# Two expert tables copied into one with 8 KB rows, fetched by one gather a pair

## The chip, the cores and the metric

The kernel runs on one core of one Trainium2 chip. The metric is the device time of one execution in microseconds; 3 runs of the kernel before are given. A core has five engines with streams of instructions of their own that meet only at semaphores: TensorE (PE, matmuls), VectorE (DVE), ScalarE (ACT), GpSimd (POOL) and SyncE (SP, which only issues transfers here). 16 DMA engines move the data.

## The reference

One sequence of 512 tokens of width 1024 in float32 goes through two blocks of layers. What is computed, in the order of the kernel:

- retention and forgetting attention, each `x = x + gate * mixer(h)`, with a modulation from `c`, and a final norm;
- a second block: `h = rms_norm(x)`, stick-breaking attention and a gated delta rule on projections of `h`, both gated and merged into `x`;
- the experts, product-key retrieval, the part that the change is about:

```python
q = einsum('bsd,de->bse', h, w_q)                    # 8 heads x 256
s1, s2 = scores of q's halves against keys1, keys2   # 128 keys each
v1, i1 = top_k(s1, 16); v2, i2 = top_k(s2, 16)
vals, c = top_k(v1[..., :, None] + v2[..., None, :], 16)
expert = i1[c // 16] * 128 + i2[c % 16]              # of 16384
gate = softmax(vals)
u = u_tab[expert]; v = v_tab[expert]                 # rows of 1024
x = x + sum_e gate_e * gelu(h . u_e) * v_e           # 128 experts a token
```

Each of the 512 tokens fetches 128 rows of the table u and 128 of the table v, 4096 B each: 537 MB in all. Both tables have 16384 rows (67 MB each).

## The kernel before

All of the kernel's stages follow one another on the whole sequence: retention, forgetting, stick breaking, the inputs of the delta rule, the delta rule, gates, merge, experts. Weights of the projections come in chunks of 512 columns, two halves of 1 MB each. `load` (L191) has SP wait until DVE has split the half before (`w_split`) and then issues the transfer into `raw[h]`; ACT makes the high part (L214), DVE the low part (L219), and PE multiplies with both (L277). `load_chunks` (L197) is a loop on SP where there are more than 4 chunks. In the blocks of the attention proper (line 1493 and on, line 1735 and on) SP has nothing to issue; in the delta rule's block only the masks (L2202).

The experts are `peer` (L2684). Tokens lie on the 128 partitions, 4 tiles of 128 tokens; the 128 experts of a token are 16 groups of 8, so there are 64 groups, and every gather fetches, for one expert place `k`, one row per partition, by an index on that partition (`eidx`). Before, a gather fetches a row of u or a row of v, 512 KB, so a group takes 16 gathers, and the stage 1024, all issued by POOL through `gather_row` (L2721). For each group:

- DVE makes 8 dot products of a u row with the token's h (L2928), 1024 wide, into `dots`;
- ACT applies gelu (L3045), DVE multiplies by the gate (L2945), ACT spreads the 8 weights into 8 diagonal matrices (L3049);
- PE multiplies each diagonal by the v row, two matmuls of 512 columns an expert, and sums all 128 experts of a tile in PSUM (`weigh`, L2830, in part a loop of rounds). Each expert counts `v_used`.

There are 16 slots for u rows and 16 for v rows, two groups of each; `u_row` and `v_row` (L2819, L2822) say where they lie, in tiles that earlier stages have left. POOL issues the 8 u gathers of group g once DVE has made the dots of group g-2 (`dot_done`), and then the 8 v gathers of group g once PE has used the rows of group g-2 (`v_used`), one after the other (`gather`, L3075). For the first two groups it waits instead for what lies in the tiles: the x stored, the last weights split, the last projection done, the last scores read.

Between the dots of the groups DVE also chooses the keys and experts of later groups (`top_keys`, `top_pairs`, `experts`, `softmax`) up to the 52nd group or so; these stand in the order of lines 2968 to 2996. The dots of the last group are made in three segments (4, 2 and 2). After each tile of tokens `add_rows` (L2948) adds the sum to x, and PE waits for that before the next tile.

## Time and profile before

| | us |
|---|---|
| median of 3 runs | 3343.18 (3341.9 to 3343.9) |
| profiled execution | 3344.73 |
| its span | 3342.9 |
| busy: PE | 2809.0 (84%) |
| busy: DVE | 1849.4 (55%) |
| busy: ACT | 884.3 (26%) |
| busy: POOL | 1216.9 (36%) |
| DMA, mean over the span | 211 GB/s |

The span reaches from the first to the last instruction; the execution's own time lies 1.8 us above it. Busy times are sums over the whole span, and the kernel's stages differ much, so they say little of one stage: the slices and windows do. L12 is line 12 of the kernel. What "idle before" is ascribed to is inferred from semaphores; where a DMA is named that ended long ago, the name says nothing. In a timeline PE's ends are modelled.

### The profile page before, as it was taken

What the parts mean: (1) busy time and instruction counts of PE and PEld (TensorE: products, weight loads), DVE (VectorE), ACT (ScalarE), POOL (GpSimd) and SP (SyncE); (2) the same over time, 40 slices, a digit from 0 to 9 for tenths busy, and PEclk for the clock granted to TensorE, in tenths of its full rate; (3) what the DMA queues carried; (4) which work ended last, traced back from release to release, by engine and by line L of the source; (5) the groups of instructions that cost most, each with busy time, mean ns of one, the idle gap of its engine ahead of it and who ended that gap; (6) DMA issues with size and microseconds to landing.
All of it is one profiled execution on the core that took longest, in us unless ns stands there. A gap on an engine that the chain in (4) does not pass through costs nothing. (4 is left out here: it accounts for less than half of the span.)

```text
span 3342.9 us, 31046 instructions
## 1 busy us (share of the span) xinstructions
PE 2809.0 (84%) x10832; PEld 1865.1 (56%) x10832; DVE 1849.4 (55%) x3524; ACT 884.3 (26%) x1621; POOL 1216.9 (36%) x1236
## 2 busy tenths in 40 slices
PE   6999999999899999999999786766776667757777
PEld 5888587765677677898778632222332222323323
DVE  4761544244534564556344676656667666757443
ACT  2112322514446564324223211111111111111111
POOL 0000210000202241540001466666666666666665
PEclk7999999999999999999999898878888878878878
DMA  6452123200221123003233799999999999999998
GB/s 235 154 186 88 63 82 96 88 26 1 87 90 63 52 89 119 1 1 115 88 111 110 264 352 370 365 370 390 371 368 364 380 368 386 353 374 382 367 369 312
DMA packets 228772, 706.47 MB, mean 211 GB/s; under 512 B 23188, under 2 KB 25492, under 8 KB 227735
## 3 DMA queue, kind: packets, MB, share of 16 engines
q0 software_dynamic: 147456, 536.94, 41.8%
q1 hardware_dynamic: 81176, 167.76, 14.6%
q8 instruction: 77, 1.26, 0.2%
q14 instruction: 63, 0.52, 0.0%
HBM read 694.13 MB, written 10.49 MB: 211 GB/s over the span
## 5 line engine op out<-in xcount | busy, mean ns | idle before, releaser
L2836 PE MATMUL work_banks<-rows_over_split,sig 128*128 128x512 f32 x1024 | 518.9, 661 | 265.7 <-issue 191.6
L2836 PEld LDWEIGHTS work_banks<-rows_over_split,sig 128*128 128x128 f32 x1024 | 214.6, 212 | 562.0 <-issue 482.3
L219 DVE TENSOR_TENSOR weights_low<-weights_raw,weights_high 128x2048 fp32r<-128x2048 f32 x108 | 250.5, 2320 | 430.4 <-ACT weights_high L214 420.9
L2836 PE MATMUL work_banks<-weights_raw,sig 128*128 128x512 f32 x512 | 266.5, 678 | 155.3 <-issue 90.9
L2928 DVE CUSTOM_DVE_ANT_0 proj_banks<-rows_over_parts,work_banks 128x1024 f32<-128x1024 f32 x256 | 309.1, 1245 | 155.5 <-DMA rows_over_parts<-in_peer_u_dram,eidx 74.6
L277 PE MATMUL proj_banks<-h_low,weights_high 128*128 128x512 f32 x896 | 357.9, 399 | 27.9 <-DVE weights_low L219 9.1
L214 ACT CAST weights_high<-weights_raw 128x2048 fp32r<-128x2048 f32 x108 | 206.0, 1907 | 610.9 <-PE proj_banks L277 582.7
L277 PE MATMUL proj_banks<-h_high,weights_low 128*128 128x512 f32 x896 | 352.7, 394 | 0.0
L277 PE MATMUL proj_banks<-h_high,weights_high 128*128 128x512 f32 x896 | 352.5, 393 | 0.0
L2722 POOL DMA_INDIRECT rows_over_split<-in_peer_v_dram,eidx x256 | 241.6, 944 | 156.2 <-issue 71.9
L2836 PEld LDWEIGHTS work_banks<-weights_raw,sig 128*128 128x128 f32 x512 | 109.3, 219 | 310.5 <-issue 245.3
L3045 ACT ACTIVATE coef<-dots 128x8 f32<-128x8 f32 x63 | 13.1, 209 | 985.2 <-issue 569.5
L2722 POOL DMA_INDIRECT rows_over_parts<-in_peer_u_dram,eidx x256 | 239.8, 937 | 79.8 <-issue 71.4
L3049 ACT ACTIVATE sig<-shape_consts,coef 128x128 f32<-128x128 f32 x504 | 154.0, 388 | 222.9 <-DVE coef L2945 117.8
L277 PEld LDWEIGHTS proj_banks<-h_low,weights_high 128*128 128x128 f32 x896 | 170.5, 190 | 66.2 <-issue 21.9
L2928 DVE CUSTOM_DVE_ANT_0 proj_banks<-u_rows_first,work_banks 128x1024 f32<-128x1024 f32 x128 | 154.8, 1254 | 69.5 <-DMA u_rows_first<-in_peer_u_dram,eidx 54.4
L277 PEld LDWEIGHTS proj_banks<-h_high,weights_low 128*128 128x128 f32 x896 | 170.8, 191 | 37.0 <-issue 1.9
L277 PEld LDWEIGHTS proj_banks<-h_high,weights_high 128*128 128x128 f32 x896 | 170.6, 190 | 36.3
L2836 PE MATMUL work_banks<-v_rows,sig 128*128 128x512 f32 x384 | 177.7, 612 | 8.0 <-issue 8.0
L277 PE MATMUL proj_banks<-weights_high,h_low 128*128 128x512 f32 x448 | 177.2, 395 | 0.0
L277 PE MATMUL proj_banks<-weights_high,h_high 128*128 128x512 f32 x448 | 174.4, 389 | 0.0
L277 PE MATMUL proj_banks<-weights_low,h_high 128*128 128x512 f32 x448 | 174.3, 389 | 0.0
(490 smaller groups left out, 4934.5 us busy)
## 6 DMA issues: line engine op xcount, KB each, us to landing
weights_raw<-in_w_in_dram SPq DMA_DIRECT2D x36, 1024.0 KB, 4.9
weights_raw<-in_ret_w_in_dram SPq DMA_DIRECT2D x24, 1024.0 KB, 5.2
ret_gate<-in_mod_w_dram SPq DMA_DIRECT2D x20, 1024.0 KB
weights_raw<-in_fox_w_in_dram SPq DMA_DIRECT2D x16, 1024.0 KB, 5.2
weights_raw<-in_ret_w_out_dram SPq DMA_DIRECT2D x8, 1024.0 KB, 5.2
weights_raw<-in_peer_w_q_dram SPq DMA_DIRECT2D x8, 1024.0 KB, 5.3
ret_v<-in_mod_w_dram SPq DMA_DIRECT2D x4, 1024.0 KB
weights_raw<-in_fox_w_out_dram SPq DMA_DIRECT2D x4, 1024.0 KB, 5.1
```

Source lines behind the costliest of these rows:

```text
L214: nc.scalar.copy(whi[h][:, :, :], raw[h][:, :, :]).then_inc(high_ready[h], 1)
L219: nc.vector.tensor_tensor(wlo[h][:, :, :], raw[h][:, :, :], whi[h][:, :, :].bitcast(F32), ALU.subtract).then_inc(w_split[h], 1)
L277: last = nc.tensor.matmul(out_tile, lhs, rhs, start=(start and j == 0), stop=(stop and j == 2))
L2722: return nc.gpsimd.indirect_dma_start(out=to, out_offset=None, in_=table, in_offset=bass.IndirectOffsetOnAxis(ap=eidx[:, t, k:k + 1].bitca ...
L2836: last = nc.tensor.matmul(pa[:, half, :], diag[:, s, e, :], v_row(s, e)[:, half * CW:(half + 1) * CW], start=(first and e == 0), stop=(las ...
L2928: nc.vector.tensor_tensor_reduce(out=trash[:, e % 2, :], in0=u_row(g % 2, e), in1=hp, scale=1.0, scalar=0.0, op0=ALU.mult, op1=ALU.add, ac ...
L3045: nc.scalar.activation(coef[:, g % 2, :], dots[:, g % 2, :], ACT.Gelu).then_inc(gelu_done, 1)
L3049: nc.scalar.activation(diag[:, g % 2, e, :], ident, ACT.Copy, scale=coef[:, g % 2, e:e + 1]).then_inc(diag_ready, 1)
```

## The change

Both tables are copied by DMA, DRAM to DRAM, into a third, `joined_rows`, whose row i is the u row and the v row of expert i side by side, 8192 B. The copy is 128 pieces of 256 rows, 1 MB each. SP issues them (`join_rows`): one behind each half of a weight load (but not in the first 8 chunks of retention), one after each step of the attention blocks and some of the delta rule's, where SP's stream has new waits for the steps of these stages. The loop of `load_chunks` is unrolled for that. POOL waits for all 128 before the first gather.

One gather then fetches both rows of an expert, 1 MB, 512 gathers in all. There are 16 slots of 8 KB per partition, in the same tiles; a slot is free again when PE has used its v half, for DVE's dots have read its u half before that. PE's weighing is written out without a loop, and its waits for `v_loaded` and ACT's waits for `v_used` go.

```diff
 
+
+JOIN_PIECES = 128
+JOIN_ROWS = PEER_KEYS * PEER_KEYS * 2 // JOIN_PIECES
...
+    joined = nc.dram_tensor("joined_rows", [PEER_KEYS * PEER_KEYS, 2 * D], F32, kind="Internal").ap()
+    state = {"g": 0, "joined": 0}
 
 
 
-    def load(sp, src, c, g):
+    def join_rows(sp, pieces=1):
+
+        for piece in range(state["joined"], min(state["joined"] + pieces, JOIN_PIECES)):
+            rows = slice(piece // 2 * JOIN_ROWS, (piece // 2 + 1) * JOIN_ROWS)
+            table = a["peer_v_2" if piece % 2 else "peer_u_2"][0]
+            sp.dma_start(joined[rows, piece % 2 * D:(piece % 2 + 1) * D], table[rows, :]).then_inc(rows_joined, 16)
+            state["joined"] = piece + 1
+
+    def load(sp, src, c, g, join=True):
 
         for h in range(2):
             sp.wait_ge(w_split[h], g + 1)
             sp.dma_start(raw[h][:, :, :], src(c, h)).then_inc(w_loaded[h], 16)
+            if join:
+                join_rows(sp)
 
     def load_chunks(sp, src, n, then=None):
 
         g0 = state["g"]
-        if n <= 4:
-            for c in range(1, n):
-                load(sp, src, c, g0 + c)
-        else:
-            with sp.Fori(0, n - 1) as i:
-                load(sp, src, i + 1, i + (g0 + 1))
+        for c in range(1, n):
+            load(sp, src, c, g0 + c)
         if then is not None:
             load(sp, then, 0, g0 + n)
...
                             late_unit(u)
                         for c in range(1, n):
-                            load(sp, ret_in_src, c, g0 + c)
+                            load(sp, ret_in_src, c, g0 + c, join=c >= 8)
                             if 4 <= c < 8:
                                 for u in range(units_before[c], units_before[c + 1]):
...
+                    @block.sync
+                    def _(sp):
+                        for m in range(PAIRS):
+                            sp.wait_ge(o_full, m + 1)
+                            join_rows(sp)
+
                     @block.tensor
...
                 with nc.Block() as block:
+                    @block.sync
+                    def _(sp):
+                        for h in range(H):
+                            sp.wait_ge(z_full, B * (h + 1))
+                            join_rows(sp)
+                            sp.wait_ge(o_full, h + 1)
+                            join_rows(sp)
+
                     @block.tensor
                     def _(pe):
...
                     sp.dma_start(masks[:, :, :], a["inv_masks"]).then_inc(masks_loaded, 16)
+                    for h in range(H):
+                        sp.wait_ge(products_full, h + 1)
+                        join_rows(sp)
+                    for g in range(NG):
+                        for lv in range(LV):
+                            sp.wait_ge(cs_ready, nth(g, lv, HG - 1))
+                            join_rows(sp)
+                    for n in range(0, TT * H, 4):
+                        sp.wait_ge(vn_full, n + 1)
+                        join_rows(sp)
                     sp.wait_ge(z_put, 16)
 
                 @block.gpsimd
...
-        u_loaded = [[sem(f"u_loaded{s}_{b}") for b in range(GE)] for s in range(2)]
-        v_loaded = [[sem(f"v_loaded{s}_{b}") for b in range(GE)] for s in range(2)]
+        pair_loaded = [[sem(f"pair_loaded{s}_{b}") for b in range(GE)] for s in range(2)]
         ur0 = sbuf(st, "u_rows_first", [P, GE // 2, D])
...
-
-        def gather_row(to, table, t, k):
+        def gather_pair(to, t, k):
             return nc.gpsimd.indirect_dma_start(
-                out=to, out_offset=None, in_=table,
+                out=to, out_offset=None, in_=joined,
                 in_offset=bass.IndirectOffsetOnAxis(ap=eidx[:, t, k:k + 1].bitcast(U32), axis=0))
 
         def top16(values, scratch, out_v, out_i):
...
             dots = sbuf(st2, "dots", [P, 2, GE])
             coef = sbuf(st2, "coef", [P, 2, GE])
-            diag = spare[:, 2:6, :].rearrange("p j (e n) -> p j e n", e=4).rearrange("p (s j) e n -> p s (j e) n", s=2)
+            diag = spare[:, 0:4, :].rearrange("p j (e n) -> p j e n", e=4).rearrange("p (s j) e n -> p s (j e) n", s=2)
             trash = pb[:, :, :].rearrange("p (e b) n -> p e (b n)", e=2)
             hp = pa[:, 2:4, :].rearrange("p b n -> p (b n)")
 
+            def pair(s, e):
+
+                flat = lambda ap: ap.rearrange("p b n -> p (b n)")
+                if s == 0 and e < 4:
+                    return flat((ur0 if e < 2 else x)[:, 2 * (e % 2):2 * (e % 2) + 2, :])
+                if s == 0 and e < 6:
+                    return flat(raw[e % 2][:, :, :])
+                if e >= 6:
+                    return flat((over_split[:, 2:4, :], over_split[:, 6:8, :], vr[:, 0:2, :],
+                                 spare[:, 4:8, :])[2 * s + e - 6])
+                row = (0, 4, 2, 6, 0, 4)[e]
+                return flat((over_parts if e < 4 else over_split)[:, row:row + 2, :])
+
             def u_row(s, e):
-                return over_parts[:, (0, 1, 4, 5, 2, 3, 6, 7)[e], :] if s else first_u_row(e)
+                return pair(s, e)[:, 0:D]
 
             def v_row(s, e):
-                if s == 0:
-                    return raw_row(e) if e < GE // 2 else over_split[:, (2, 3, 6, 7)[e - GE // 2], :]
-                if e < 4:
-                    return over_split[:, (0, 1, 4, 5)[e], :]
-                return vr[:, e - 4, :] if e < GE - 1 else spare[:, 6:8, :].rearrange("p b n -> p (b n)")
+                return pair(s, e)[:, D:2 * D]
 
             with nc.Block() as block:
-                def weigh(pe, r, s, t, first, last_of_tile):
+                def weigh(pe, t, g):
 
                     for e in range(GE):
-                        pe.wait_ge(diag_ready, r * (2 * GE) + (t * NG * GE + s * GE + e + 1))
-                        pe.wait_ge(v_loaded[s][e], r * 16 + 16 * (t * NG // 2 + 1))
+                        pe.wait_ge(diag_ready, (t * NG + g) * GE + e + 1)
                         for half in range(2):
-                            last = nc.tensor.matmul(pa[:, half, :], diag[:, s, e, :],
-                                                    v_row(s, e)[:, half * CW:(half + 1) * CW],
-                                                    start=(first and e == 0),
-                                                    stop=(last_of_tile and e == GE - 1))
+                            last = nc.tensor.matmul(pa[:, half, :], diag[:, g % 2, e, :],
+                                                    v_row(g % 2, e)[:, half * CW:(half + 1) * CW],
+                                                    start=(g == 0 and e == 0),
+                                                    stop=(g == NG - 1 and e == GE - 1))
                         last.then_inc(v_used, 1)
 
...
@@ -2890,13 +2926,8 @@
                     for t in range(TT):
                         if t:
                             pe.wait_ge(y_added, t)
-                        weigh(pe, 0, 0, t, True, False)
-                        weigh(pe, 0, 1, t, False, False)
-                        with rounds(pe, NG // 2 - 2) as r:
-                            for s in range(2):
-                                weigh(pe, r + 1, s, t, False, False)
-                        weigh(pe, NG // 2 - 1, 0, t, False, False)
-                        weigh(pe, NG // 2 - 1, 1, t, False, True)
+                        for g in range(NG):
+                            weigh(pe, t, g)
 
                 @block.vector
                 def _(dve):
...
                     def scores_of(t, g, rows=(0, GE)):
 
                         for e in range(*rows):
-                            dve.wait_ge(u_loaded[g % 2][e], 16 * ((t * NG + g) // 2 + 1))
+                            dve.wait_ge(pair_loaded[g % 2][e], 16 * ((t * NG + g) // 2 + 1))
 
                             dve.wait_ge(dot_done, (t * NG + g) * GE + (PRE + e - 1))
...
@@ -3022,6 +3053,12 @@
                         nc.scalar.copy(sc[:, t, 4 * n - 4:4 * n, :],
                                        pa[:, t, :].rearrange("p (f c) -> p f c", c=P)).then_inc(sc_ready, 1)
 
+                    def diagonals(n_of, lo=0, hi=GE):
+
+                        for e in range(lo, hi):
+                            nc.scalar.activation(diag[:, n_of % 2, e, :], ident, ACT.Copy,
+                                                 scale=coef[:, n_of % 2, e:e + 1]).then_inc(diag_ready, 1)
+
                     for t in range(TT):
                         for g in range(NG):
                             n_of = t * NG + g
...
@@ -3031,11 +3068,7 @@
                                     nc.scalar.activation(coef[:, g % 2, lo:hi], dots[:, g % 2, lo:hi], ACT.Gelu
                                                          ).then_inc(gelu_done, 1)
                                     act.wait_ge(coef_ready, n_of + 1 + segment)
-                                    if segment == 0:
-                                        act.wait_ge(v_used, n_of * GE + GE)
-                                    for e in range(lo, hi):
-                                        nc.scalar.activation(diag[:, g % 2, e, :], ident, ACT.Copy,
-                                                             scale=coef[:, g % 2, e:e + 1]).then_inc(diag_ready, 1)
+                                    diagonals(n_of, lo, hi)
                                 continue
                             if n_of == 3:
                                 exponentials(0, 1)
...
@@ -3044,54 +3077,30 @@
                             act.wait_ge(dot_done, n_of * GE + (PRE + GE))
                             nc.scalar.activation(coef[:, g % 2, :], dots[:, g % 2, :], ACT.Gelu).then_inc(gelu_done, 1)
                             act.wait_ge(coef_ready, n_of + 1)
-                            act.wait_ge(v_used, n_of * GE + GE)
-                            for e in range(GE):
-                                nc.scalar.activation(diag[:, g % 2, e, :], ident, ACT.Copy,
-                                                     scale=coef[:, g % 2, e:e + 1]).then_inc(diag_ready, 1)
+                            diagonals(n_of)
 
                 @block.gpsimd
                 def _(pool):
                     pool.wait_ge(eidx_ready, 1)
-                    for e in range(GE):
-                        if e == GE // 2:
-                            pool.wait_ge(x_put, 16)
-                        gather_row(first_u_row(e), u_tab, 0, e).then_inc(u_loaded[0][e], 16)
-                    for e in range(GE // 2):
-                        if e % 2 == 0:
-                            pool.wait_ge(w_split[e // 2], state["g"] + n + 1)
-                        gather_row(raw_row(e), v_tab, 0, e).then_inc(v_loaded[0][e], 16)
-                    pool.wait_ge(first_used, state["g"] + n + 1)
-                    for e in range(GE // 2, GE):
-                        gather_row(v_row(0, e), v_tab, 0, e).then_inc(v_loaded[0][e], 16)
-                    for e in range(GE):
-                        if e == GE // 2:
-                            pool.wait_ge(tile_full[3], state["g"] + n + 1)
-                        gather_row(u_row(1, e), u_tab, 0, GE + e).then_inc(u_loaded[1][e], 16)
-                    for e in range(GE):
-                        if e == GE // 2:
-                            pool.wait_ge(s_full, 4 * n)
-                        gather_row(v_row(1, e), v_tab, 0, GE + e).then_inc(v_loaded[1][e], 16)
-
-                    def gather(table, g, s, used, loaded, rows=(0, GE)):
-
-                        t, first = g // NG, (g % NG) * GE
-                        if table is u_tab and g == NG // 4:
+                    pool.wait_ge(rows_joined, 16 * JOIN_PIECES)
+                    freed = {(0, 2): (x_put, 16), (0, 4): (w_split[0], state["g"] + n + 1),
+                             (0, 5): (w_split[1], state["g"] + n + 1), (0, 6): (first_used, state["g"] + n + 1),
+                             (1, 2): (tile_full[3], state["g"] + n + 1), (1, 6): (s_full, 4 * n)}
+                    for g in range(2):
+                        for e in range(GE):
+                            if (g, e) in freed:
+                                pool.wait_ge(*freed[g, e])
+                            gather_pair(pair(g, e), 0, g * GE + e).then_inc(pair_loaded[g][e], 16)
+                    for g in range(2, LAST + 1):
+                        if g == NG // 4:
                             pool.wait_ge(eidx_ready, 2)
-                        elif table is u_tab and g == NG // 2:
+                        elif g == NG // 2:
                             pool.wait_ge(eidx_ready, 3)
-                        elif table is u_tab and g > NG // 2 and g % 2 == 0:
+                        elif g > NG // 2 and g % 2 == 0:
                             pool.wait_ge(eidx_ready, 3 + g // 2 - NG // 2 + 1)
-                        for e in range(*rows):
-                            pool.wait_ge(used, g * GE + (e + 1))
-                            gather_row(u_row(s, e) if table is u_tab else v_row(s, e), table, t, first + e
-                                       ).then_inc(loaded[s][e], 16)
-
-                    for g in range(2, LAST):
-                        gather(u_tab, g, g % 2, dot_done, u_loaded)
-                        gather(v_tab, g, g % 2, v_used, v_loaded)
-                    for rows in SEGMENTS:
-                        gather(u_tab, LAST, LAST % 2, dot_done, u_loaded, rows)
-                        gather(v_tab, LAST, LAST % 2, v_used, v_loaded, rows)
+                        for e in range(GE):
+                            pool.wait_ge(v_used, g * GE + (e + 1))
+                            gather_pair(pair(g % 2, e), g // NG, (g % NG) * GE + e).then_inc(pair_loaded[g % 2][e], 16)
             stage_end(n)
 
     then_out = columns(a["fox_w_out"][0])
```

## Rows read from the trace of the kernel before

**Rows 1.** The page's busy tenths, 40 slices of 83.6 us.

```profile
PE   6999999999899999999999786766776667757777
...
DMA  6452123200221123003233799999999999999998
```

**Rows 2.** The page's DMA queues: packets, MB, share of 16 engines' span.

```profile
q0 software_dynamic: 147456, 536.94, 41.8%
q1 hardware_dynamic: 81176, 167.76, 14.6%
```

**Rows 3.** Windows of the expert stage: busy us (instructions) by engine, PEclk, DMA share, GB/s.

```profile
1930.00:2430.00 500.00, 351.57 (x724) 148.60 (x723) 334.76 (x821) 67.74 (x211) 332.11 (x354) 0.84 0.97 372
2430.00:2930.00 500.00, 348.84 (x711) 147.78 (x712) 328.77 (x827) 68.60 (x214) 330.75 (x351) 0.83 0.96 370
...
3080.00:3310.00 230.00, 175.70 (x350) 71.80 (x348) 106.24 (x179) 29.19 (x99) 153.38 (x165) 0.84 0.97 372
```

**Rows 4.** Line L3045 (gelu) in 1950:3050 and 3080:3310: count, duration, first and last start.

```profile
L3045 ACT ACTIVATE coef<-dots x49: 208/208/210, 1954.7 to 3036.0; 128x8 f32<-128x8 f32 x49
...
L3045 ACT ACTIVATE coef<-dots x11: 208/208/210, 3080.7 to 3296.9; 128x8 f32<-128x8 f32 x11
```

**Rows 5.** Waits of DVE, 1950:3050: total us, times, longest.

```profile
DVE peer_vals L2728 <- DMA sb_gains<-in_sb_q_norm_w_dram: 34.1, 7, 5.3
...
DVE peer_v L2731 <- DMA sb_gains<-in_sb_q_norm_w_dram: 32.2, 9, 5.0
...
DVE peer_vals L2728 <- issue: 23.1, 5, 5.3
...
DVE peer_vals L2731 <- DMA sb_gains<-in_sb_q_norm_w_dram: 18.0, 5, 4.0
```

**Rows 6.** Waits of DVE, 3080:3310.

```profile
DVE proj_banks L2928 <- DMA rows_over_parts<-in_peer_u_dram,eidx: 65.5, 6, 14.8
DVE proj_banks L2928 <- DMA u_rows_first<-in_peer_u_dram,eidx: 54.4, 6, 13.2
```

**Rows 7.** Timeline of DVE, one choice of top pairs: start, us, what, idle before.

```profile
2411.68 0.42 DVE L2741 TENSOR_TENSOR peer_cand<-peer_v 128x256 f32<-128x256 f32 x1
2417.41 0.43 DVE L2728 MAX8 peer_vals<-peer_cand 128x8 f32<-128x256 f32 x1 [5.31 <-DMA sb_gains<-in_sb_q_norm_w_dram]
...
2423.03 0.43 DVE L2731 MAX8 peer_vals<-peer_cand 128x8 f32<-128x256 f32 x1 [3.33 <-DMA sb_gains<-in_sb_q_norm_w_dram]
...
2427.91 0.17 DVE L2945 TENSOR_TENSOR coef<-coef,egate 128x8 f32<-128x8 f32 x1 [3.00 <-issue]
```

**Rows 8.** Waits of POOL, 1950:3310.

```profile
POOL rows_over_split L2722 <- PE work_banks L2836: 42.8, 16, 5.4
```

**Rows 9.** Windows of the first groups.

```profile
1905.00:1920.00 15.00, 0.00 (x0) 0.00 (x0) 10.51 (x19) 0.21 (x1) 11.30 (x13) 0.50 1.03 418
1920.00:1925.00 5.00, 3.71 (x5) 1.65 (x6) 1.83 (x10) 2.45 (x8) 0.00 (x0) 0.50 1.03 421
1925.00:1930.00 5.00, 5.00 (x12) 2.08 (x11) 4.72 (x16) 0.00 (x0) 2.32 (x3) 0.85 0.65 206
```

**Rows 10.** Timeline of POOL, first groups.

```profile
1919.03 0.94 POOL L2722 DMA_INDIRECT x_res<-in_peer_u_dram,eidx  x1 [0.30 <-remote]
```

**Rows 11.** Timeline of PE, first group.

```profile
1921.29 9.71 PE L2836 MATMUL work_banks<-weights_raw,sig 128*128 128x512 f32 x16 [21.44 <-issue]
```

**Rows 12.** Line L195, the weight loads to 1850 us.

```profile
L195 SPq DMA_DIRECT2D weights_raw<-in_w_in_dram x36: 367/368/1107, 864.7 to 1589.5; - x36
...
DMA to landing us min/median/max: 4.7/5.1/13.8
```

**Rows 13.** The page's costliest groups, ACT's casts of weights.

```profile
L214 ACT CAST weights_high<-weights_raw 128x2048 fp32r<-128x2048 f32 x108 | 206.0, 1907 | 610.9 <-PE proj_banks L277 582.7
```

**Rows 14.** Timeline of PE, the end.

```profile
3331.55 5.31 PE L2836 MATMUL work_banks<-v_rows,sig 128*128 128x512 f32 x12
3336.70 1.88 PE L2836 MATMUL work_banks<-sig 128*128 128x512 f32 x4
```

10 lines of the change are left out of this document (3 added, 7 removed).

## The prediction

> **What bounds the kernel now.** I read the page's slices first. The span falls into two parts: up to about 1850 us TensorE is at 9 tenths and DMA at 0 to 5; from 1850 us to the end DMA stands at 9 tenths, while PE and DVE stand at 6 or 7 [rows 1]. The second part is the expert stage, 45% of the span, and all of the change's work is there, but for the copies that feed it. The reader is to see in the queue table that the gathers (q0) alone took 41.8% of the 16 DMA engines' span, and that a packet of the other queue (q1) is about half as long [rows 2].
>
> The windows then say how evenly the stage runs: 370 to 372 GB/s at a DMA share of 0.96 or 0.97, all the way [rows 3]. That looks like a stage that DMA sets alone. The pace of the groups of eight experts says more. One gelu a group: 49 of them from 1954.7 to 3036.0 us, which is 48 steps of 22.53 us, and 11 from 3080.7 to 3296.9 us, 10 steps of 21.62 us [rows 4]. What a group costs DMA is q0's time over the gathers: 41.8% of 16 x 3342.9 us is 22,357 us; by 1024 gathers and 16 engines 1.365 us a gather; sixteen gathers a group, 21.84 us. So in the last stretch the rows set the pace (DVE waits there for landings, 65.5 and 54.4 us [rows 6]), but in the 48 groups before it hardly: in 1100 us DVE's list has no wait for a landing of rows among the longest, and its gaps have other names [rows 5]. DVE is busy 334.76 of 500 us there [rows 3], 15.1 us of each 22.53, and the other 7.4 us are gaps inside its own chain: 5.31 us between a tensor_tensor and the max8 behind it, then 3.33 us, then 3.00 us, in one choice of top pairs [rows 7]. These gaps carry names of DMAs that ended long ago, so what they wait for is not known; they do not occur in the list of the last stretch [rows 6]. In that middle DVE and DMA are within 0.7 us of each other, and POOL, which needs 0.94 us and 0.30 us between two gathers [rows 10], 16 x 1.24 = 19.8 us a group, is not far off either and loses 42.8 us in its longest kind of wait for PE [rows 8]. Three engines are nearly level; that decides what speeding up one can give.
>
> **The change, part by part.**
>
> Packets. A gather of pairs moves 128 rows of 8192 B where two moved 256 of 4096 B. From the two queues: a q0 row costs its engine 1.365/8 = 170.6 ns with its share of the closing packets; q1 14.6% of 53,486 us over 81,176 packets, 96.2 ns for 2067 B on average [rows 2]. A line through both has 36.7 ns per 1000 B and 20.4 ns fixed. 8192 B would take 320.8 ns against 341.2: 64 of them per engine and group, 1.3 us less, 20.5 us a group. The other bound is no fixed part, or rows cut in two: 21.8 us. I take 21.0, as q1's mean holds small packets that inflate the fixed part.
>
> The last stretch (12 groups) goes by DMA: from 21.62 to 21.0, -7 us.
>
> The middle (48 groups). DVE's dots, choices of keys and weights are unchanged, eight dots and the same chores. If DVE alone sets it, 22.53 stays; if DMA alone does, 21.0. POOL's 512 instructions fewer take it out of the race: 8 x 1.24 = 10 us a group. Against that, a slot's u half is no longer given back at the dot but only when PE has used the v half; before, eight gathers (11 us of transfer) of the group after next could be issued while DVE was still busy with chores. I take 22.1, near DVE's end: 48 x 0.43 = -21 us. Bounds 20.5 and 22.5 by the rows, above that the rival below.
>
> The first groups. Before, POOL ran on with eight u gathers (the last at 1919.0 us [rows 10]) while PE had not yet used anything; the queue ran at 418 to 421 GB/s until 1925 us, and only then fell to 206 for 5 us [rows 9]. Now the 16 pair slots are full when POOL has issued what was 32 gathers, and the next pair waits for PE's first use at 1921.3 us [rows 11]. Eight gathers of 1.25 us (0.524 MB at 418 GB/s) move behind that, +10 us, less the 2.5 us that the dip cost: +7.5; DVE has chores then that cover a part. I take +6, bounds 0 and +10.
>
> The copies. 128 pieces of 1 MB, DRAM to DRAM, 1 MB each behind a weight load or a step of a mixing stage. No such copy is in the trace. By its reads alone one takes 1.05 MB/418 GB/s = 2.5 us, if reads and writes add up 5 us. The load behind it lands then at 7.6 to 10.1 us where it landed at 5.1 [rows 12]. ACT's casts waited for PE 582.7 us over 108 times, 5.4 us each, of 610.9 us of idle time in all [rows 13]: on average the copy is hidden, by PE's use of the tiles before. Also the unrolled loops on SP issue the same loads. The copies are spread by load, and by my count 86 are issued before the delta rule, where DMA's slices are 0 and 2 tenths, 30 in it, and the last near 1660 us, 190 us before the first gather; the wait for them is free. I take +4; bounds 0 and +40 (15 loads without slack, 2.5 us each).
>
> The end. Before, PE's last 16 matmuls begin at 3331.55 us with the landing of v rows, 12 of 5.3 us and 4 of 1.9 us to the end [rows 14]. After, the last pair's landing is followed by dot 1.3, gelu, weight and diagonal about 1.0, 4 matmuls 1.9: -2 us. PE's unrolled weighing has its waits for rows dropped, since the diagonal follows the dot on the same pair: 0.
>
> Sum: -7 - 21 + 6 + 4 - 2 = -20, from the profiled execution's 3344.7 us to 3324.7. That execution lies 1.5 us above the median shown, so 3323.
>
> A rule of the Trainium skill (DMA: Bandwidth & Descriptors, Queues, rings and completion order) says that each engine turns between rings only after a whole packet of descriptors. Pairs double the bytes of such a turn. It speaks against this change, for whatever else must come through the same engines; no row here shows what DVE's gaps wait for, so it gives no number by itself and only stands beside the third rival.
>
> **The rivals.**
>
> 1. DMA sets the pace throughout, at 20.5 us, as POOL's load halves and DVE's gaps shrink with it. For: DVE has 7.4 idle us a group, and POOL's waits for PE. Against: DVE hardly waited for landings in the middle. 48 x 2.03 = -97, 12 x 1.1 = -13, +6, -2, the copies hidden: 3344.7 - 106 = 3239. [...]
>
> 2. DVE stays the limit at 22.53 in the middle: -7 + 6 + 4 - 2, 3346. If rows of 8 KB also go as two packets, 3353.
>
> 3. Slower: DVE's long gaps are waits for something that comes through the DMA engines and must wait behind rows; with rows twice as long and a fuller queue they grow. For: they occur only in the stage with DMA at 9 tenths, and the long ones come back at 5.3 us again and again. The gaps under those names sum to 34.1 + 32.2 + 23.1 + 18.0 = 107 us in the middle [rows 5]. Doubled, all of it shows, as DVE is the limit: +107, and the +1 of rival 2: 3453; at half of that 3400. It decides as soon as DVE's group goes over 22.5 us. Held-back slots work the same way: each late weight leaves DMA idle, since no u gather fills the gap.
>
> 4. The copies are not hidden: +40 in place of +4, 3360.
>
> **How the numbers follow.** Forecast 0.30, DMA everywhere 0.17, DVE unchanged 0.22, longer gaps 0.25, copies 0.06. Predicted 3323 us; the forecast's own range is 3300 to 3340. Over all cases 3237 to 3428, which leaves out a tenth on either side. 0.2% is about 7 us, what a measurement here can tell from no change. Faster by more: 0.26 of the forecast, 0.17, 0.04 from rival 2 and 0.02 from mild forms of the third: 0.49. Within: 0.15. Slower: 0.36.
>
> **What would show it.** Steps of the gelu in the profile after: 22.1 us in the middle and 21.0 at the end; 20.5 in both is rival 1, 22.5 rival 2, 24 or more rival 3. q0's share: 512 gathers, 65,536 row packets, near 40%; if 131,072, the rows were cut. DMA's share in the middle falls below 0.96 if DVE sets the pace. A hole of some 10 us in DMA before PE's first use. DVE's gaps of 5.3 us: gone, the same, or 10. The first gather must come at 1846 us; if it comes later the copies cost that much. What would make it wrong: gaps of DVE that depend on POOL's or DMA's load in a way these rows don't show.

## The result, and the profile after

The changed kernel took 3215.7 us (median of 4 runs, 3213.8 to 3219.8) beside 3343.5 us for the kernel before (3341.9 to 3349.7): ratio 0.9616, 95% interval 0.9599 to 0.9633. Forecast were 3323 us and a range of 3237 to 3428; the time lies 21 us under its low end, beyond even the first rival (3239). Three later measurements, on chips 14, 10 and 12, gave ratios of 0.9597, 0.9590 and 0.9587. One thing must be known to read the numbers below: the experiments were run on five later occasions, and on one of them the kernel before itself ran at 3211.2 us (20 runs, 3203.8 to 3217.1), on the others at 3350 to 3355 (medians), each time with all its runs; an experiment is therefore compared with the kernel before of its own occasion, or the text says that it isn't.

The page of the changed kernel first, the slices (80.3 us each) and the queues, which answer to [rows 1, 2]:

```profile
PE   6999999999899989999999988777777777787787
...
DMA  6474064521545664543833359999999999999997
...
q0 software_dynamic: 73728, 536.90, 40.4%
q1 hardware_dynamic: 115992, 301.98, 27.4%
```

The gathers move the same bytes in half as many packets (65,536 of them rows, so the rows were not cut in two), in 1298 us of each engine's time (40.4% of 3212.7) where it was 1397. The copies are seen twice: q1 has 134 MB more, and the DMA slices before the experts stand mostly at 3 to 6 where most stood at 0 to 3.

The windows of the expert stage (busy us and instructions of PE, weight loads, DVE, ACT and POOL; granted clock, DMA share, GB/s), as in [rows 3]; the last line is the stretch of the first groups:

```profile
1930.00:2430.00 500.00, 390.71 (x801) 165.39 (x802) 376.31 (x923) 76.22 (x239) 187.62 (x200) 0.89 1.00 418
2430.00:2930.00 500.00, 387.99 (x783) 164.08 (x782) 369.11 (x911) 73.20 (x229) 182.52 (x195) 0.88 1.01 415
2930.00:3180.00 250.00, 196.07 (x404) 83.03 (x404) 139.97 (x256) 36.42 (x118) 95.11 (x102) 0.90 1.01 421
1930.00:1945.00 15.00, 14.52 (x31) 6.49 (x32) 14.55 (x40) 2.44 (x8) 6.10 (x7) 0.88 0.71 273
```

DMA went from 370 GB/s to 418 at a share of 1.00, DVE does 376 us of work in 500 where it did 335, and POOL issues 200 gathers where it issued 354. The gelu's steps, one a group, against [rows 4]:

```profile
L3078 ACT ACTIVATE coef<-dots x49: 208/209/210, 1961.9 to 2937.1; 128x8 f32<-128x8 f32 x49
...
L3078 ACT ACTIVATE coef<-dots x12: 208/208/210, 2957.0 to 3178.0; 128x8 f32<-128x8 f32 x12
```

48 steps of 20.32 us (before 22.53) and 11 of 20.09 (before 21.62). The list of DVE's waits, 1950 to 3050 us, stands against [rows 5]:

```profile
DVE proj_banks L2959 <- DMA rows_over_split<-joined_rows,eidx: 130.3, 104, 2.2
DVE proj_banks L2959 <- DMA rows_over_parts<-joined_rows,eidx: 45.5, 50, 2.2
...
DVE proj_banks L2959 <- DMA u_rows_first<-joined_rows,eidx: 3.7, 4, 1.2
```

All its lines are landings of rows, none longer than 2.3 us. The choice of top pairs, whose three gaps of [rows 7] took 11.6 us together, now runs through:

```profile
2425.57 0.42 DVE L2769 TENSOR_TENSOR peer_cand<-peer_v 128x256 f32<-128x256 f32 x1
2426.03 0.43 DVE L2756 MAX8 peer_vals<-peer_cand 128x8 f32<-128x256 f32 x1
...
2427.41 0.43 DVE L2759 MAX8 peer_vals<-peer_cand 128x8 f32<-128x256 f32 x1
...
2428.40 0.17 DVE L2976 TENSOR_TENSOR coef<-coef,egate 128x8 f32<-128x8 f32 x1
```

So the gain is not mainly that rows come faster; a kind of pause inside VectorE's own work has gone. From the first gelu shown to the last are 60 group steps in both traces (a few fall between the two windows), 1342.2 and 1216.1 us: 126.1 of the 130.2 us by which the two spans differ.

What it cost is ahead of the experts. Among the waits of 1120 to 1150 us are these two, and the first of them again in the kernel before:

```profile
ACT w_ba_split L2111 <- DMA w_ba<-in_w_in_dram: 16.1, 1, 16.1
...
PE work_banks L2010 <- DMA conv_rows<-in_gdn_conv_w_dram: 6.6, 1, 6.6
...
ACT w_ba_split L2086 <- DMA w_ba<-in_w_in_dram: 2.0, 1, 2.0
```

The second wait is not in the list of the kernel before. TensorE's matmuls on the peer keys (L2905, in the kernel before L2869) tell the whole delay, by their first and last start, after and before:

```profile
L2905 PE MATMUL work_banks<-peer_keys_t,sig x128: 270/275/348, 1840.7 to 1915.9; 128*128 128x128 f32 x128
L2869 PE MATMUL work_banks<-peer_keys_t,sig x128: 270/275/348, 1823.6 to 1899.6; 128*128 128x128 f32 x128
```

Everything up to there is 17 us late. Single traces scatter: of the five without copies these matmuls begin at 1822.0 to 1830.3 us, of the twelve with all copies in place at 1837.1 to 1848.3.

### The profile page after: what moved, and what is told of

It is laid out like the page before. It is cut to its first block and busy times, and to the rows that moved or that the text cites. A ratio compares the mean times of both kernels' runs of the same rounds, so it can differ in the third digit from the quotient of the medians.

```text
span 3212.7 us, 29678 instructions
## 1 busy us (share of the span) xinstructions
PE 2807.6 (87%) x10832; PEld 1866.5 (58%) x10832; DVE 1859.5 (58%) x3524; ACT 884.8 (28%) x1621; POOL 734.8 (23%) x724
## 3 DMA queue, kind: packets, MB, share of 16 engines
q0 software_dynamic: 73728, 536.90, 40.4%
## 5 line engine op out<-in xcount | busy, mean ns | idle before, releaser
L2872 PE MATMUL work_banks<-rows_over_parts,sig 128*128 128x512 f32 x512 | 294.6, 740 | 170.7 <-ACT sig L3059 170.7
L2872 PEld LDWEIGHTS work_banks<-rows_over_parts,sig 128*128 128x128 f32 x512 | 120.2, 242 | 345.0 <-ACT sig L3059 197.6
L2872 PE MATMUL work_banks<-u_rows_first,sig 128*128 128x512 f32 x256 | 159.3, 780 | 118.4 <-ACT sig L3059 102.9
L2959 DVE CUSTOM_DVE_ANT_0 proj_banks<-rows_over_split,work_banks 128x1024 f32<-128x1024 f32 x128 | 157.3, 1231 | 150.1 <-DMA rows_over_split<-joined_rows,eidx 150.1
L2872 PE MATMUL work_banks<-rows_over_split,sig 128*128 128x512 f32 x512 | 230.2, 592 | 0.0
L2750 POOL DMA_INDIRECT rows_over_parts<-joined_rows,eidx x128 | 120.0, 938 | 347.8 <-PE work_banks L2872 337.9
L2959 DVE CUSTOM_DVE_ANT_0 proj_banks<-rows_over_parts,work_banks 128x1024 f32<-128x1024 f32 x128 | 155.7, 1239 | 63.8 <-DMA rows_over_parts<-joined_rows,eidx 63.0
L2872 PEld LDWEIGHTS work_banks<-u_rows_first,sig 128*128 128x128 f32 x256 | 61.1, 250 | 215.1 <-ACT sig L3059 133.2
L2872 PEld LDWEIGHTS work_banks<-rows_over_split,sig 128*128 128x128 f32 x512 | 97.3, 190 | 122.4 <-issue 122.4
```

Of the source, the lines that this page charges most:

```text
L2750: return nc.gpsimd.indirect_dma_start(out=to, out_offset=None, in_=joined, in_offset=bass.IndirectOffsetOnAxis(ap=eidx[:, t, k:k + 1].bitc ...
L2872: last = nc.tensor.matmul(pa[:, half, :], diag[:, g % 2, e, :], v_row(g % 2, e)[:, half * CW:(half + 1) * CW], start=(g == 0 and e == 0), ...
L2959: nc.vector.tensor_tensor_reduce(out=trash[:, e % 2, :], in0=u_row(g % 2, e), in1=hp, scale=1.0, scalar=0.0, op0=ALU.mult, op1=ALU.add, ac ...
```

## Experiments

There were eighteen runs. They test three theories: the gain comes from the longer rows (T1), from the smaller number of gathers that GpSimd issues (T2), or from the slots, the order and the unrolled weighing (T3). A "pause" below is idle time of VectorE inside its own chain of instructions, or of GpSimd ahead of a gather, that no work still running explains.

**Rows apart, in the slots of pairs.** Everything of the change but the copies and the long rows.

```
for half, (table, loaded) in enumerate(((u_table, u_loaded), (v_table, v_loaded))):
    indirect_dma_start(out=to[:, half*D:(half+1)*D], in_=table, ...).then_inc(loaded[s][e], 16)
```

> The changed kernel with its 16 pair slots, its order and its unrolled weighing, but without the copies: the u row and the v row of an expert are fetched by two gathers of 4 KB from their own tables, one behind the other into the two halves of the slot. 16 gathers of 128 rows a group, as before. If the gain lies in the slots, the order or the unrolled weighing, the groups stay near 20.3 us and the time falls by the copies' 17 us too: 3199. If it lies in the row length or in the number of gathers, VectorE's gaps of 3 to 5 us are back, a group takes about 22.5 us and the time is 3340 to 3360. I expect the second.

3361.1 us against 3353.7 (ratio 1.0017, 1.0004 to 1.0030). VectorE's pauses are back; a group takes 22.7 us (43 steps of the gelu):

```profile
L3077 ACT ACTIVATE coef<-dots x44: 208/209/210, 1965.6 to 2941.2; 128x8 f32<-128x8 f32 x44
...
DVE peer_vals L2754 <- DMA sb_gains<-in_sb_q_norm_w_dram: 15.0, 6, 3.2
```

T3 is out: with 16 gathers a group, slots, order and unrolled code give nothing, and the u half held back costs next to nothing.

**Small gathers added.** The changed kernel, with long rows, and 16 gather instructions a group again.

```
+ indirect_dma_start(out=bits[0:2, m % 16], in_=masks, in_offset=eidx[0:2, t, k]).then_inc(bit_loaded[m % 16], 16)
  indirect_dma_start(out=to, in_=joined, in_offset=eidx[:, t, k])
```

> The changed kernel, with a second indirect gather ahead of each pair gather that fetches 4 bytes for each of 2 partitions: 16 gathers a group again, but 8 of 8 KB rows and 8 of next to nothing. If VectorE's gaps come with the number of gather instructions, they are back and a group takes about 22.5 us: 3345 to 3360. If they come with the number of rows that are fetched (2048 a group before, 1024 now) or with the row length, a group stays at 20.3 us: 3216, within 10. I expect the second with 0.6.

3375.6 us against 3353.7 (1.0071, 1.0051 to 1.0091): I had expected the other outcome. Eight gathers of 8 bytes each undo the whole gain. Its gelu and its first window:

```profile
L3087 ACT ACTIVATE coef<-dots x44: 208/208/210, 1972.8 to 2948.8; 128x8 f32<-128x8 f32 x44
...
1930.00:2430.00 500.00, 349.92 (x706) 148.40 (x707) 334.66 (x823) 68.61 (x214) 318.23 (x346) 0.83 0.93 364
```

43 steps of 22.70 us, and DVE, POOL and GB/s close to [rows 3], with rows of 8 KB. The pauses are in its chain of linked steps again, 1.0 to 1.1 us ahead of instructions of 0.1 to 0.3 us (the idle time before each stands in brackets):

```profile
2424.97 0.30 DVE L2768 MAX8 peer_v<-peer_sc 128x8 f32<-128x128 f32 x1 [1.09 <-issue]
2426.36 0.09 DVE L2769 MATCH_VALUE_LOAD peer_i<-peer_v,peer_sc 128x8 f32 x1 [1.09 <-DVE peer_v L2768]
...
2427.76 0.17 DVE L2985 TENSOR_TENSOR coef<-coef,egate 128x8 f32<-128x8 f32 x1 [1.04 <-DVE peer_i L2769]
```

This settles T2 against T1: rows of 8 KB don't keep the gain when 16 gathers a group are back. A second measurement, on another chip:

> The changed kernel with a small gather ahead of each pair gather: 3375.6 on the first chip, with VectorE's pauses. If the number of gathers and the chip must come together for a pause, this is 3225 (3216 to 3240) on a chip without them (16 x 1.22 us = 19.5 us of issue under the 20.3 us of DMA), and 3375 on one with them.

3379.1 against 3350.0 us, and 3219.7 for the changed kernel beside it.

**Copies alone, and no copies.** The first is the kernel before with the 128 copies and the wait for the last of them.

> The kernel before with the 128 copies added and the gathers waiting for the last of them; the gathers still fetch 4 KB rows from the two tables, so the copies serve nothing. By the trace of the changed kernel the stages ahead of the experts end 17.0 us later, 10.9 at the first weights of the experts: 3344 + 11 to 17 = 3355 to 3361. If the delay came from something else in the changed kernel, or is absorbed in the waits of the first groups: 3344 to 3350.

3370.4 against 3353.7 us: +16.7, at the upper end of the 11 to 17 expected. The second is the changed kernel without them:

```
- in_=joined                      + in_=u_table seen as 8192 rows of 2*D
- tensor_copy(eidx, ef)           + tensor_scalar(eidx, ef, 0.5, -0.25, mult, add)
```

> The changed kernel without the copies: the 8 KB rows are fetched straight from the first table seen as 8192 rows, by halved indices (the second table is never read). All else as in the changed kernel. If the copies cost the 17.0 us that the stages ahead end later, the time is 3216 - 17 = 3199, and the groups stay at 20.3 us. If the joined table's own place in memory is better or worse for the gathers than the original's, the groups move from 20.3 us, and the time with it.

3201.2 us; the changed kernel took 3215.7 to 3219.7 on its four occasions: 14.5 to 18.5 us less, from different occasions. So the copies cost about 17 us, and nothing else in the early stages is seen to cost anything. Its gelu is also the trace of 8 KB rows on the occasion on which the kernel before had no pauses: 49 steps of 20.32 us.

```profile
L3074 ACT ACTIVATE coef<-dots x50: 208/209/210, 1950.2 to 2946.1; 128x8 f32<-128x8 f32 x50
```

**Copies moved.** The 18 copies that stood near small loads are issued in the delta rule.

```
  for h in range(H):              # stick breaking
+     if h >= 5: continue
- load(...)                       + load(..., join=c > 2)      # delta_inputs
- load(...)                       + load(..., join=False)      # gates
- join_rows(sp)                   + join_rows(sp, 2)           # delta rule, among others
```

> The changed kernel with 18 of the 128 copies moved: none beside the last three heads of the stick breaking, none beside the first two chunks of the next stage's loads (where a small load of 64 KB took 14 us longer), none in the gates stage; the 18 are issued in the delta rule, where the DMA share was 0.45. If the small loads behind copies are what costs 17 us, the stages ahead lose 2 to 4 us in place of 17, and the time is 3216 - 13 = 3203 (3200 to 3207). If the delta rule becomes late by the added copies, it is 3216 or more.

3202.9 us beside 3353.7: ratio 0.9551 (0.9533 to 0.9569). It was measured twice more, both times beside the changed kernel:

> The changed kernel with the 18 copies moved, beside the changed kernel on one chip: 3202.9 before on a chip with pauses; nothing in it depends on them, so 3203 on any chip (3199 to 3208), 13 under the changed kernel, and on a chip without pauses also under the kernel before by 8.

3208.9 beside the changed kernel's 3219.7;

> The version with 18 copies moved: 3203 to 3209, 0.3 to 0.4% under the changed kernel on the same chip. On a chip without pauses also under the kernel before (3211): ratio 0.997 to 1.000.

3207.5 (0.9557, 0.9542 to 0.9573) beside 3215.9 (0.9587, 0.9571 to 0.9602), five rounds: 8 to 11 us less. The peer keys' first use comes at 1830.8 us in its trace and at 1847.0 in the changed kernel's of the same occasion. On these three occasions this version beats both kernels.

**The loop on TensorE written out, in the kernel before.** This, the kernel without copies and the next two shared the occasion on which the kernel before took 3211.2 us.

> The kernel before with one edit of the change alone: TensorE's loop over the middle groups is written out. If jumps or register waits on TensorE held the ring of slots back, some of the 2.2 us a group come with it (3340 down to 3290). If the gather instructions alone do, nothing moves: within 5 us of before. I expect the second.

3212.0 against 3211.2: nothing, on an occasion without pauses. But it is the trace that shows the kernel before (but for that loop) without its pauses. A window, and the gelu:

```profile
1930.00:2430.00 500.00, 388.43 (x805) 165.15 (x806) 380.08 (x918) 76.68 (x241) 378.39 (x400) 0.89 1.03 413
...
L3045 ACT ACTIVATE coef<-dots x49: 208/208/210, 1964.5 to 2945.8; 128x8 f32<-128x8 f32 x49
```

400 gathers of 4 KB rows in 500 us at 413 GB/s: 48 steps of 20.44 us. That is what rows of 4 KB and 16 gathers a group can do where nothing pauses, 0.12 us behind the 20.32 of the kernels with pairs. Over all 60 steps it took 1226.1 us, and the changed kernel 1216.1. So the long rows, with the slots, are worth 10 us in all; the kernel without copies also lies 10 us under the kernel before of this occasion.

**One row in place of two.** The changed kernel with 8 gathers of 4 KB a group.

```
- out=to, in_=joined              + out=to[:, 0:D], in_=u_table
- v_row = pair[:, D:2*D]          + v_row = pair[:, 0:D]
```

> The changed kernel without the copies, and each of the 8 gathers of a group fetches one row of 4 KB from the first table; TensorE weighs that same row in place of the second table's (half of the data is left out). DMA then has half the bytes, so it bounds nothing. If VectorE's pauses come with the row length (4 KB rows bad, 8 KB rows good), they are back: 20 to 22 us a group. If they come with the number of gathers, VectorE runs through its own work, 376 us busy of each 500 at 20.3 us a group, so 15.3 us, and with the waits behind the end of each group's chain 15.5 to 17.5 us a group: 64 groups x 3.5 us less, 3199 - 224 = 2975 (2910 to 3060). I expect the second.

2863.6 us; less even than the 2910 to 3060 expected. Its first window:

```profile
1930.00:2430.00 500.00, 467.88 (x1062) 201.93 (x1062) 485.24 (x1213) 98.91 (x309) 251.51 (x265) 0.98 0.81 283
```

VectorE works 485 of 500 us. Against the kernel without copies it is 338 us less, 5.3 us a group, so 15.0 us a group. That is what VectorE's own work sets; my forecast had taken the 22.53 us with its pauses in them.

**Half the dose.** One small gather ahead of every second pair gather, 12 a group.

```
+ if m % 2 == 0:
      indirect_dma_start(out=bits[0:2, m % 16], ...)
```

> As the kernel with the small gathers (3375.6 us), but with one ahead of every second pair gather: 12 gather instructions a group, between the 8 (20.3 us) and the 16 (22.5 us and more). If what counts is GpSimd's own time to issue them, 12 x 1.24 us = 14.9 us a group lies under the 20.3 us that DMA needs, and the time stays within 10 us of 3216. If each gather holds VectorE back by itself, half of the way is lost: 3280 to 3310. I expect the first with 0.55.

3220.1 us here, and on an occasion where the kernel before had its pauses:

> 12 gathers a group (a small one ahead of every second pair gather): 3220.1 on the chip without pauses. On a chip with them: if a pause needs GpSimd's queue to be full nearly all of a group's time (16 x 1.24 = 19.9 of 20.3 us), 14.9 us of issue leave it out: 3220 to 3230. If each gather carries a pause, half of the 16 gathers' loss is there: 3290 to 3310.

3221.8 against 3354.1, with 297 gathers in 500 us and DVE at 373:

```profile
1930.00:2430.00 500.00, 388.73 (x798) 164.92 (x799) 373.45 (x910) 74.85 (x234) 275.26 (x297) 0.89 1.00 414
```

The changed kernel took 3215.7 us beside it. So 12 gathers a group cost 6 us, and 16 cost 160 where pauses occur. The loss is not in proportion to the gathers; it sets in between 14.9 and 19.8 us of issue a group (at 1.24 us each), where DMA allows 20.3.

**GpSimd busy with something else.** Four fills ahead of each pair gather.

```
+ for i in range(4):
+     wait_ge(bits_set, 4 * (t*HK + k) + i); memset(bits, 0.0).then_inc(bits_set, 1)
```

> The changed kernel with four small fills (128x144) by GpSimd ahead of each pair gather: 8 gathers a group as in the changed kernel, but GpSimd busy for most of a group. On a chip with pauses: if any work of GpSimd beside VectorE's makes the pauses, they are back and a group takes over 21.5 us (3290 to 3380); if only gathers do, 3216 to 3230. On a chip without pauses it says only that GpSimd's time lies under DMA's: 3216 to 3230, or more if 8 gathers and 32 fills need over 20.3 us.

3217.7 us beside the changed kernel's 3219.7. Its window:

```profile
1930.00:2430.00 500.00, 387.59 (x793) 164.26 (x794) 377.03 (x915) 74.85 (x234) 359.95 (x985) 0.88 1.00 417
```

GpSimd is busy for 360 of 500 us, more than in the kernel before (332 [rows 3]), and nothing pauses. It isn't the engine's being busy.

**Small copies by SyncE.** Eight transfers a group more, on the other queue.

```
+ sp.wait_ge(v_used, m + 1)
+ sp.dma_start(bits[m % 16], u_table[0:16, 0:16]).then_inc(bit_loaded[m % 16], 16)
```

> The changed kernel with 8 small copies of 1 KB a group added (16 rows of 64 bytes, DRAM to DRAM, one for each pair that TensorE has used), issued by SyncE on the hardware queue: 16 transfers a group end with their counts again, as before, but GpSimd issues 8 gathers only. On a chip with pauses: if they come with the number of transfers that end and count up semaphores, they are back and the time is 3290 to 3390; if they come with GpSimd's gathers alone, it is 3216 to 3235. On a chip without pauses it is 3216 to 3235 either way. I expect the second with 0.6.

3218.9 against 3354.1 us:

```profile
1930.00:2430.00 500.00, 395.54 (x800) 167.45 (x800) 374.35 (x913) 74.86 (x235) 187.86 (x200) 0.88 1.01 416
...
bits<-in_peer_u_dram SPq DMA_DIRECT2D x394, 1.0 KB, 5.1
```

The second line is from the list of DMA issues of 1950 to 2950 us: 394 small copies, 5.1 us from issue to landing, beside the gathers. So it isn't the number of transfers that end and count, at least not when SyncE issues half of them.

**Small gathers, half the bytes.** 16 gathers a group, but DMA with time to spare.

```
  indirect_dma_start(out=bits[0:2, ...])
- indirect_dma_start(out=to, in_=joined)      + out=to[:, 0:D], in_=u_table
```

> The kernel with the small gathers (16 gathers a group, 3375 to 3379 us on chips with pauses), but each pair gather fetches 4 KB from the first table only, and TensorE weighs that row too (half of the data left out; the copies stay). DMA has half the bytes. GpSimd's issue then sets the pace: 16 x 1.22 = 19.5 us a group, so about 64 x 0.8 = 50 us less than the 3216 of the changed kernel: 3165 to 3200 if no pauses come. If 16 gathers a group bring the pauses by themselves, it stays at 3300 to 3380 on a chip with them. I expect the pauses, with 0.6.

3376.5 against 3355.0 us. The same time as with all the bytes:

```profile
L3087 ACT ACTIVATE coef<-dots x44: 208/209/210, 1954.2 to 2932.4; 128x8 f32<-128x8 f32 x44
...
1950.00:2450.00 500.00, 352.61 (x718) 148.88 (x716) 332.10 (x807) 67.09 (x208) 323.25 (x353) 0.84 0.64 187
```

43 steps of 22.75 us at a DMA share of 0.64. So the bytes play no part in the 22.5 us. GpSimd's issue alone, 0.94 us a gather and 0.30 to the next, makes 19.8 of them; the rest is pauses, of VectorE in its own chain and of GpSimd ahead of a gather. The longest sums of the two in 1000 us (us in all, times, longest), each under the name of a load that ended long ago:

```profile
POOL bits L2755 <- DMA x_res<-in_mod_b_dram: 105.4, 37, 6.8
...
DVE peer_vals L2768 <- DMA sb_gains<-in_sb_q_norm_w_dram: 17.8, 4, 4.7
```

Spread over the gathers the pace is 1.42 us each, but that is a mean with pauses in it and no price of one gather. This run was made on the chip on which the kernel before had run without pauses, so the pauses don't belong to a chip, as my expectations put it: chip 12 showed both.

**The changed kernel again.** Three times beside the kernel before, in the hope of an occasion without pauses.

> The changed kernel once more, beside the kernel before on one chip. On the chip of the last call the kernel before took 3211.2 us, 132 less than on the first: there VectorE has none of the long pauses in its own work (10.9 us of gaps in 980, of which all are missing records, against 285), with the same 16 gathers. If the pauses belong to some chips, there are two outcomes: on a chip with them before 3343 to 3360 and the changed kernel 3216 (ratio 0.96); on one without them before 3211 and the changed kernel 3216 to 3219, because DMA holds both at 20.1 to 20.3 us a group and the copies add 17 (ratio 1.001 to 1.003).

> The changed kernel beside the kernel before once more. On a chip with pauses before 3343 to 3360 and the ratio 0.96, as twice; on one without, before 3211 and the changed kernel 3216 to 3220, ratio 1.001 to 1.003.

> The changed kernel: 3216 to 3220; ratio 0.96 on a chip with pauses, 1.001 to 1.003 on one without.

Ratios 0.9597 (0.9571 to 0.9623), 0.9590 (0.9566 to 0.9615), 0.9587. All three occasions had the pauses. What the change is worth without them was not measured directly. Argued from the parts, it is a loss of some 7 us: 3211.2 for the kernel before, 3201.2 for the changed kernel without copies, to which the copies' 17 us come. The changed kernel with half the dose took 3220.1 there.

## Why the prediction was wrong

Right was where it looked: three engines nearly level, with the name of the unknown in its last sentence ("gaps of DVE that depend on POOL's or DMA's load in a way these rows don't show"). Wrong was the step "I take 22.1, near DVE's end".

- **The middle, 48 groups, -21 us.** Measured 22.53 to 20.32: -106. The step read DVE's 7.4 us of gaps a group as part of its pace, as they didn't carry a name that could be believed. The runs show that (but for one occasion) they come with 16 gathers a group, and that they are gone with 12 or 8. "POOL's 512 instructions fewer take it out of the race" was counted as issue time, 16 x 1.24 = 19.8 us, which fits under everything, and given the value 0; it was the whole effect. The first rival had the mechanism ("as POOL's load halves and DVE's gaps shrink with it"), with 0.17. Its own size was off too: 20.5 us a group, and copies hidden.
- **Packets, 1.3 us a group at most.** The rows of 8 KB came at 20.32 us, the lower bound of 20.5 or a little under. But what was compared with it, 21.84 us from q0's share, was not a DMA limit: where nothing paused, 4 KB rows came at 20.44. Their packets took less time there too, 1335 us of each engine (41.6% of 3208.1, the row below) where it was 1397 for the same gathers. A queue's packet time in a stage that also waits elsewhere is no price of a packet. The difference by row length is 0.12 us a group in the middle, 10 us over all 60 steps.

```profile
q0 software_dynamic: 147456, 536.94, 41.6%
```

- **The last stretch, 12 groups, -7 us.** "So in the last stretch the rows set the pace." 20.09 came for 21.0; from the end of the middle to the last gelu shown, 12 steps, it was 260.9 us before and 240.9 after: -20. DMA was not the limit there either: in the loop experiment's trace the same rows came at 20.5 in this stretch (11 steps). Before, GpSimd's 165 gathers of 230 us [rows 3] need 205 us at 1.24 each, so it was issuing nearly all the time; that its pauses made the landings of [rows 6] late fits this, but was not tested for that stretch.
- **The first groups, +6 us.** The hole is there, but small: in 1930 to 1945 us the DMA share is 0.71, so 4.4 us are lost. From the first matmul on the peer keys to the first gelu shown it took 131.1 us before, 121.2 after, and 120.0 in the loop experiment's trace without pauses. So the 10 us that the start of the stage gave back are pauses gone, and the held-back slots cost 1 at most.
- **The copies, +4 us.** Measured 16.7 alone. The average slack of ACT's casts was the wrong row: the loss stands at small loads that no cast waits for, w_ba and conv_rows, behind copies of 1 MB and beside them (the wait is 14 us longer, the work behind it 9.3 us late), in the delta rule (1.5) and in the gates (6.1). The bounds, 0 to 40, held it. "The first gather must come at 1846 us" came at 1863.3.
- **The end, -2 us.** From the last gelu shown to the end of the span 46.0 us before, 34.7 after: -11. The loop experiment's trace, without pauses, has 36.8. So some 2 us are the change, as forecast, and 9 are pauses gone from the last group.
- **Third rival, longer gaps (0.25).** It had the gaps wait for something that comes through the DMA engines. With DMA at a share of 0.64 the longest ahead of a max8 is 5.0 us, where it was 5.3 at 0.96, and the group takes as long: not so. Rows of twice the length didn't lengthen them either; beside the small gathers the longest was 4.0. In both runs fewer of them stand in VectorE's chain than before, so the pace there follows GpSimd more than VectorE.

The sum by measured parts, on the two profiled executions: 60 steps -126.1, the start +7.2, the end -11.3, together -130.2.

The Trainium skill (Perfetto Trace Analysis, DMA Optimizations) puts the overhead at transfers under 2 KB and says that batching them into 4 or 8 KB can improve throughput dramatically. It doesn't set 4 KB against 8; here that step gave 1%: 413 GB/s with rows of 4 KB where nothing paused, 418 with 8. No run here fetches its rows in smaller pieces.

Open is what a pause is. It occurs at waits for counts that were due: of VectorE for its own step before, of GpSimd ahead of a gather, under the name of a DMA that ended long ago. What holds these counts up isn't shown, nor why one occasion was free of it. The traces with pauses hold few of the gathers' landings: for the gathers of 1950 to 2950 us the loop experiment's trace has this row, and that of the kernel before has none:

```profile
DMA to landing us min/median/max: 9.3/25.5/33.2
```

All six traces with pauses hold 5962 to 7859 landing records; the loop experiment's holds 19,322 for the same gathers, and the one with SyncE's small copies 19,312. With 12 gathers a group the trace of the pause-free occasion has 17,274, the other 11,792, though nothing paused there: records go missing before time does. My guess is that something that carries counts or their records is overfull when gathers follow each other without rest. A rival stands untested: that the recording itself makes the pauses. Each time on record comes with a span and a clock from the profiler, so no run shows what either kernel takes without it, nor whether the 4% would be there. The Trainium skill (SBUF — State Buffer, Who interferes with whom) offers a lock: an instruction of VectorE with two inputs in SBUF and one of GpSimd that reads SBUF exclude each other for a whole instruction. The pause of 5.31 us in [rows 7] does follow such an instruction, but GpSimd's last 0.94 us each, and twelve of them a group hold nobody back; no run here shows the lock.

## What to carry to other kernels

Count the gathers of GpSimd as a resource of its own: 12 in a group of 20.3 us cost next to nothing, and 16 set the pace on all occasions but one, at 1.42 us each on average, not at the 1.24 us between two issues. A gap inside an engine's own chain, ended by a name that can't be the cause, is a number that may vanish: forecast both with and without it, before anything else is weighed. And work that is slipped in beside loads (copies here) must be priced at the smallest load that somebody waits for, not by the mean slack of the big ones; moving 18 of 128 copies took back 8 to 11 of 17 us.

## What was not expected of the hardware

- The same program ran at 3211 us and at 3344 to 3355 us, all runs of an occasion alike, and on chip 12 once in each way. A comparison that doesn't share the occasion can invent or hide 4%.
- Eight gathers of 8 bytes a group cost 160 us (3219.7 to 3379.1 on one occasion); half as many cost 6 (3215.7 to 3221.8); 32 fills of 128x144 a group cost nothing.
- Copies from DRAM to DRAM: 128 of 1 MB beside the early stages cost 17 us, 15 of it at two places, though in stretches like 1090 to 1150 us they hold the DMA share at 0.95 to 1.03.
